# The order of turns, products and copies in the mixer stages of a two-layer encoder kernel

## What is computed

```python
def _chunk_relpos_core(q, k, v, q_pos, k_pos, valid, table):   # layer 0, mixer A, 8 heads
    s = jnp.einsum('bcqhd,bckhd->bchqk', q, k) * ATTN_SCALE + bias[None, None]
    p = jax.nn.softmax(jnp.where(valid[None, :, None, None, :], s, NEG_INF), axis=-1)
    return jnp.einsum('bchqk,bckhd->bcqhd', p, v)

def _diff_core(q, k, v, q_pos, k_pos, lam, slopes):            # layer 0, mixer B, 4 double heads
    s = jnp.einsum('bqhid,bkhid->bhiqk', q, k) * ATTN_SCALE - slopes * dist
    p = jax.nn.softmax(jnp.where(vis, s, NEG_INF), axis=-1)
    return jnp.einsum('bhqk,bkhd->bqhd', p[:, :, 0] - lam * p[:, :, 1], v)

def _forget_core(q, k, v, dq, dk, q_pos, k_pos):               # layer 1, mixer C, 16 heads
    s = jnp.einsum('bqhd,bkhd->bhqk', q, k) * ATTN_SCALE + dq - dk
    p = jax.nn.softmax(jnp.where(k_pos <= q_pos, s, NEG_INF), axis=-1)
    return jnp.einsum('bhqk,bkhd->bqhd', p, v)

proj = h @ w_in      # gives q, k and v of each head; k and v are outputs too (new cache rows)
out  = concat(heads) @ w_out
```

## Time and profile before

| | before |
|---|---|
| median of 3 runs | 2443.89 us (2441.65 to 2446.6) |
| profiled execution | 2447.24 us |
| its span on the core | 2445.4 us |
| mean granted TensorE clock | 0.987 of 2.4 GHz |
| PE busy | 2337.1 us (96% of the span) |
| DVE busy | 1443.2 us (59%) |
| ACT busy | 907.9 us (37%) |

### The profile page before, as it was taken

How to read it: one execution, slowest core, us unless ns; L and a number is a source line. 1 busy time by engine, 2 the same in 40 slices (tenths; PEclk the granted TensorE clock), 3 DMA queues, 4 the chain that set the end, 5 groups by cost and what they waited for, 6 DMA issues and landing times.

```text
span 2445.4 us, 45688 instructions
## 1 busy us (share of the span) xinstructions
PE 2337.1 (96%) x18984; PEld 2224.9 (91%) x18984; DVE 1443.2 (59%) x2606; ACT 907.9 (37%) x1964; POOL 305.0 (12%) x369
## 2 busy tenths in 40 slices
PE   7999999999997999999999999997999899999998
PEld 4999999978776999999999999996777789999998
DVE  4577757655557756657575665756555576543223
ACT  4322232455555422223342222334555564222232
POOL 0000002411103400001220000233011151000001
PEclk9999999999998999999999999998999999999999
DMA  7455546322222135445524454542233221432321
GB/s 244 125 165 172 165 131 169 102 71 74 76 64 75 51 114 154 139 136 153 143 61 130 138 156 130 154 124 64 79 98 98 81 87 53 138 104 87 97 85 56
DMA packets 392701, 277.68 MB, mean 114 GB/s; under 512 B 11104, under 2 KB 349824, under 8 KB 392496
## 3 DMA queue, kind: packets, MB, share of 16 engines
q1 hardware_dynamic: 385792, 254.77, 35.5%
q0 software_dynamic: 6704, 19.99, 2.8%
HBM read 263.48 MB, written 12.81 MB: 113 GB/s over the span
## 4 chain that ended last, share of the span: by engine, by line
PE 83%; DVE 8%; ACT 3%; issue 3%; DMA 2%; POOL 1%; SPq 0%; ACTq 0%; DVEq 0%; POOLq 0%
PE lin L1018 61%; PE lin L1275 9%; PE lin L1038 2%; PE ps_s L1325 2%; PE ps_o L1397 2%; PE ps_t L1346 1%; DVE neg_max L2416 1%; DVE acc L1981 1%; DMA raw<-in_ffn_w_down 1%; DVE x L2066 1%; DVE probs L2408 1%; PE ps_s L1094 1%; DVE sums L2028 1%; DVE h_lo L2093 1%; ACT w_hi L1513 0%
## 5 line engine op out<-in xcount | busy, mean ns | idle before, releaser
L1018 PE MATMUL lin<-h_hi,w_hi 128*128 128x272 f32 x2640 | 566.4, 289 | 4.0 <-ACT work L1593 2.1
L1018 PE MATMUL lin<-h_hi,w_lo 128*128 128x272 f32 x2640 | 563.6, 289 | 0.0
L1018 PE MATMUL lin<-h_lo,w_hi 128*128 128x272 f32 x2640 | 561.5, 288 | 0.0
L1942 DVE TENSOR_TENSOR w_lo<-raw,w_hi 128x1024 fp32r<-128x1024 f32 (+1 forms) x263 | 320.5, 1223 | 309.8 <-ACT w_hi L1513 308.1
L1018 PEld LDWEIGHTS lin<-h_hi,w_hi 128*128 128x128 f32 x2640 | 421.2, 188 | 6.6 <-ACT work L1593 2.8
L1018 PEld LDWEIGHTS lin<-h_lo,w_hi 128*128 128x128 f32 x2640 | 421.6, 189 | 0.0
L1018 PEld LDWEIGHTS lin<-h_hi,w_lo 128*128 128x128 f32 x2640 | 418.9, 189 | 0.0
L1513 ACT ACTIVATE w_hi<-raw 128x1024 fp32r<-128x1024 f32 (+1 forms) x263 | 270.1, 1037 | 182.5 <-DMA raw<-in_ffn_w_down 143.5
L1981 DVE SCALAR_TENSOR_TENSOR acc<-raw,silu_c,acc 128x512 f32<-128x512 f32 x448 | 314.0, 759 | 0.0
L1018 PE MATMUL lin<-act_hi,w_hi 128*128 128x272 f32 x1296 | 285.1, 290 | 5.6 <-DVE w_lo L1942 5.3
L1018 PE MATMUL lin<-act_lo,w_hi 128*128 128x272 f32 x1296 | 283.0, 289 | 0.0
(11 more groups left out here) (313 smaller groups left out, 3461.1 us busy)
## 6 DMA issues: line engine op xcount, KB each, us to landing
raw<-in_w_ada SPq DMA_DIRECT2D x128, 512.0 KB, 3.9
raw<-in_ffn_w_gate SPq DMA_DIRECT2D x88, 512.0 KB, 3.9
raw<-in_ffn_w_up SPq DMA_DIRECT2D x88, 512.0 KB, 3.8
raw<-in_ffn_w_down SPq DMA_DIRECT2D x64, 448.0 KB, 4.3
raw<-in_ffn_w_down SPq DMA_DIRECT2D x32, 512.0 KB, 5.0
raw<-in_w_in_ab SPq DMA_DIRECT2D x24, 512.0 KB, 3.8
raw<-in_w_in_c SPq DMA_DIRECT2D x24, 512.0 KB, 3.8
start_w<-in_w_ada SPq DMA_DIRECT2D x16, 512.0 KB, 12.0
```

What stands on the lines that cost most here:

```text
L1018: m = nc.tensor.matmul(out[a], w_tile(w, k), mv[:, k0 + k, half(a)], start=first and k == 0 and n == 0, stop=last and k == u["tiles"] - 1 ...
L1942: nc.vector.tensor_tensor(w_all(w_l, u["tiles"]), raw_all(u, w_l), w_all(w_h, u["tiles"]).bitcast(F32), ALU.subtract).then_inc(lo_done, 1)
```

## The change

Three things change, in the order of instructions alone; no instruction is added, removed or resized.

1. In stages 1 to 7 the turns go from the start of steps 5, 9 and 12 to the end of steps 5, 9 and 11, on PE and on ACT. On PE a turn now stands behind the step's product, softmax transposes and value products. On ACT its copies now stand behind the step's `out_hi`, `inv_copy` and `empty_probs`, ahead of its exponential; for the rest that puts them ahead of step 12 and so of `evac(2)`, the copy of qT.
2. `tr_plan` counts the turn behind the softmax block of the same step.
3. In stage 0 the turn of v goes to bank `ps_o`, without a wait for `tr_out`; the turn of the rest then waits only for the copy of k.

```diff
+TURN_STEPS = (5, 9, 11)
@@ tr_plan
             for s in range(STEPS + 2):
-                if st.new is not None and s in (5, 9, 12):
-                    found.append((s, "turn"))
                 j = s - lag
                 if st.att is not None and 0 <= j < 10 and (st.att != "b" or j % 2):
                     found.append((s, "probs"))
+                if st.new is not None and s in TURN_STEPS:
+                    found.append((TURN_STEPS.index(s), "turn"))
             return found
+        def turn_bank(st, i):
+            return ps_o if st.st == 0 and i == 1 else ps_t
@@ PE, turn
-                    n = tr_plan(st).index((step, "turn"))
-                    wait_tr(base + n)
-                    if step in (5, 9):
+                    n = tr_plan(st).index((i, "turn"))
+                    if turn_bank(st, i) is ps_t:
+                        wait_tr(base + (1 if st.st == 0 and i == 2 else n))
+                    if i < 2:
                         for t in range(QT):
-                            m = nc.tensor.transpose(ps_t[:, t * P:(t + 1) * P], src[:, t * P:(t + 1) * P], ident[:])
+                            m = nc.tensor.transpose(turn_bank(st, i)[:, t * P:(t + 1) * P], src[:, t * P:(t + 1) * P],
+                                                    ident[:])
@@ PE, a step
-                    if st.new is not None and s in (5, 9, 12):
-                        turn(s)
...
                     if att != "b" and 0 <= j < 10 and j % 2:
                         pair_values(j // 2)
+                    if st.new is not None and s in TURN_STEPS:
+                        turn(TURN_STEPS.index(s))
                     if s < 10 and s % 2 == 0:
                         scores(s)
                         scores(s + 1)
@@ ACT, a step
                     if st.new is not None:
                         if s in (4, 8, 12):
                             evac(s // 4 - 1)
-                        if s in (5, 9, 12):
-                            empty_turn(s)
...
                     if 0 <= j < 10 and j % 2 and att == "b":
                         b_square(j // 2)
+                    if st.new is not None and s in TURN_STEPS:
+                        empty_turn(TURN_STEPS.index(s))
                     if s < 10:
                         exps(s)
```

More of the change, by code:

```diff
@@ L1414, in stage @@
                         m.then_inc(fl_ps, 1)
-                    for s in (5, 9, 12):
-                        turn(s)
+                    for i in range(3):
+                        turn(i)
                     return
                 for s in range(STEPS + 2):
-                    if st.new is not None and s in (5, 9, 12):
[L1421 to L1431, removed]
+                    if st.new is not None and s < LIN_STEPS:
+                        lin_chunk(s, 0)
+                        lin_chunk(s, 1)
+                    if st.st == 8 and s in OUT_PART[st.kind]:
+                        m, k = OUT_PART[st.kind][s]
+                        if k == 0:
+                            pe.wait_ge(kv_evac, evs)
+                        if k == max(OUT_PART[st.kind].values())[1]:
+                            pe.wait_ge(o_lo_done, st.at("ot"))
+                        out_part(st.j, m, k)
                     j = s - lag
@@ L1793, in first_stage @@
                 split(("q", j, 1, 0))
-                for s in (5, 9, 12):
-                    empty_turn(s)
+                for i in range(3):
+                    empty_turn(i)
             def forget_act():
@@ L1813, in evac, with empty_turn @@
                                          scale=HD ** -0.5 if k == 2 else 1.0).then_inc(kv_evac, 1)
-                def empty_turn(step):
-                    n = plan_t.index((step, "turn"))
+                def empty_turn(i):
+                    n = plan_t.index((i, "turn"))
                     act.wait_ge(tr_ps, st.at("tr") + n + 1)
-                    if step in (5, 9):
-                        if step == 5:
+                    if i < 2:
+                        if i == 0:
                             act.wait_ge(kv_stored[st.new], 64 * st.same_new)
-                        dst = (k_nat if step == 5 else v_nat)[:, st.new, 0:QT, :].rearrange("p t n -> p (t n)")
-                        nc.scalar.activation(dst, ps_t[:, :], ACT.Copy).then_inc(tr_out, 1)
+                        dst = (v_nat if i else k_nat)[:, st.new, 0:QT, :].rearrange("p t n -> p (t n)")
+                        nc.scalar.activation(dst, turn_bank(st, i)[:, :], ACT.Copy).then_inc(tr_out, 1)
                     else:
@@ L1832, in empty_probs @@
                         act.wait_ge(pv_done, st.at("pv") + (q - 1 if att == "b" else q // 2))
+                    dst = probsT[:, q % 2]
                     if t < QT:
-                        nc.scalar.activation(probsT[:, q % 2, 0:t + 1, :].rearrange("p b n -> p (b n)"),
+                        nc.scalar.activation(dst[:, 0:t + 1, :].rearrange("p b n -> p (b n)"),
                                              ps_t[:, 0:(t + 1) * P], ACT.Copy).then_inc(tr_out, 1)
                     else:
-                        nc.scalar.activation(probsT[:, q % 2, 0:2, 0:DEC],
+                        nc.scalar.activation(dst[:, 0:2, 0:DEC],
                                              ps_t[:, 0:2 * P].rearrange("p (b n) -> p b n", b=2)[:, :, 0:DEC], ACT.Copy)
-                        nc.scalar.activation(probsT[0:DEC, q % 2, 2, 0:DEC], ps_t[0:DEC, 2 * P:2 * P + DEC], ACT.Copy)\
+                        nc.scalar.activation(dst[0:DEC, 2, 0:DEC], ps_t[0:DEC, 2 * P:2 * P + DEC], ACT.Copy)\
                             .then_inc(tr_out, 1)
```

8 lines of the change are left out of this document (4 added, 4 removed).

## The result

| | before | after |
|---|---|---|
| median of 11 runs each | 2444.9 us | 2452.67 us |
| lowest and highest | 2441.65 to 2448.11 | 2445.78 to 2463.28 |
| profiled execution | 2447.24 us, granted clock 0.987 | 2460.93 us, granted clock 0.984 |

The ratio is 1.0036 with a 95% interval of 1.0023 to 1.0049: the change makes the kernel slower, by 7.8 us from median to median. The forecast was 2452.0 with a range of 2444.5 to 2459. The profiled execution lies above that range, which is a first hint that something varies from run to run.

The account below looks back on a forecast made before the run. PE, busy 96% of the span, was taken to bound the kernel. Terms +4.8 + 7.4 - 4.6 - 0.9 = +6.7 us on the median 2443.89 gave 2450.6; one clock fall of 1.7 made 2452, range 2444.5 to 2459.

Parts of the forecast that it names:

- The ends: Ends of "a" and "c" stages: next product waits for qT, copied later; +0.69 us at ten, +0.5 at one, +7.4 in all.
- Steps 5 and 9: In 11 "a" and "c" stages: turns wait for the `probsT` copy, +0.22 us per step, +4.8 in all.
- ACT's lateness: Step 5 of "a" and "c" stages: ACT reaches its copy only at 1788.17, behind a weight split begun at 1787.65.
- "b" stages: Stages 2, 4, 6 of layer 0: the wait ahead of the turn of k goes, 3 x 1.53, -4.6 us.
- Stage 0: Layer 0: turn of v no longer waits for `k_nat`, next product starts earlier, -0.9 us; layer 1: 0.
- The sum at full clock: Whole kernel, four order terms without any added clock fall: +6.7 us, giving 2450.6 on the median.
- The clock: Ends of "a" and "c" stages: a longer stretch of short work and waits may let the granted clock fall, 1.7 us each.
- one fall of the clock, 1.7, which is likelier than none: Added to the 2450.6 us of the order terms: a single fall of the granted clock, 1.7 us, giving 2452.
- The rival at 2459: A third to a half of the 11 "a" and "c" ends lose clock, +7 to +8 us, about 2459; chance 0.17.
- a mean clock under 0.98: Sign in the measured profile: mean clock below 0.98 would put the rival of many clock falls first.
- Steps free: Steps 5 and 9 of "a" and "c" cost nothing, as earlier `o_hi` repays: sum +1.9, 2446 us; chance 0.15.
- the loop through `o_hi`: Earlier `o_hi` at steps 5 and 9 paces "a" and "c" stages, gaining 10.6 us: sum -8.7, 2435; chance 0.08.

Follow-up runs that it names:

- Experiment 5: Kernel before with only ACT's copies of the turned rest put ahead of qT's copy at stage ends, one bank: 2455.78 us, ratio 1.0038.
- experiment 1: Changed kernel with ACT's copy of qT put back ahead of the three copies of the turned rest: 2442.89 us, ratio to before 0.9993.
- experiment 4: Kernel before with only the turns of k and v in "a" and "c" stages moved to the end of steps 5 and 9: 2449.19 us, ratio 1.0017.
- filled kernel: Changed kernel plus four unused matmuls on PE behind the last value products of "a" and "c" stages, filling the wait for qT: 2450.77 us, ratio 1.0025.
- experiment 6: The changed kernel again, unaltered, on another chip, against the kernel before: 2456.46 us, ratio 1.0040.
- experiment 2: Kernel before with only the "b" stages' turns of k and v moved to the end of steps 5 and 9, single bank in stage 0: 2437.41 us, ratio 0.9974.
- experiment 8: Kernel before with ACT's k and v copies at the end of steps 4 and 8 in "a"/"c", changed "b" stages and stage 0 bank: 2419.18 us, ratio 0.9891.

## Why the prediction was right, and where it was not

**The ends: right.** Predicted +0.69 each. Experiment 5, with nothing else changed, has +0.72, and experiment 1, with nothing else taken back, -0.73. At stage 7 of layer 0 and behind the last "c" stage waits of 0.6 stand, where 0.5 and 0.69 were forecast. The durations came out of the trace's rows; by the formula of the Trainium skill ("ScalarE: Activation LUTs", section "What ACT_TABLE_LOAD costs") the term was 0.84, and the measured 0.72 to 0.73 decides for the rows. With ten ends and a half it is +7.7 against +7.4.

**Steps 5 and 9: right.** Predicted +0.44 for a stage, measured 0.40 (experiment 4), so +4.4 against +4.8. The turn of k waits 1.13, where 1.1 to 1.3 was said. The copy of 384 columns takes 0.47, estimated at 0.49. With the two terms a "c" stage was to last 35.9 us, and at full clock it lasts 35.87. One reading was too short: the prediction puts ACT's lateness on the weight split ahead of the copy, but ahead of both stood an exponential that waited 1.26 us for DVE's `neg_max`. In the change it waits the same 1.26 us, so the sum did not suffer.

**"b" stages: right.** -1.51 measured, -1.53 predicted for a stage. The kernel with that part alone is 6.8 faster where 4.6 was forecast; the interval holds both, and one or two falls fewer would fill the gap.

**Stage 0: right.** From the turn of k to the next product it is 497.87 - 494.95 = 2.92 us, before 3.85: -0.9. In layer 1 the wait for `decay` did grow, to 4.2 us.

**The sum at full clock** is thus 4.4 + 7.7 - 4.5 - 0.9 = +6.7, the forecast's own value. The filled kernel measures that sum without the falls at the ends: 0.0025 of 2444.25 is +6.1 (3.9 to 8.3).

**The clock: right mechanism, mis-sized term.** The step "one fall of the clock, 1.7, which is likelier than none" treated falls as rare and separate. A fall costs 37.41 - 35.87 = 1.54 us, close to 1.7. Their number is what was off: 0, 3, 6 and 6 at the six counted ends of layer 1. By the ratios the change costs about 8.8 us (0.0036 of 2444.9), 2 to 3 more than the 6.1 of the filled version; from median to median it is 7.8 and 6.5. On the chip of experiment 6 the change cost 9.8 by the ratio. So I estimate the share of the clock at 1 to 4 us, and that the 1.7 falls into it is in part luck: it was one fall, and there are none or several. The intervals of 1.0036 and 1.0025 overlap, so the size of the clock's share in the median is an estimate. That PE standing still at the end lets the clock fall rests on counts of "c" stages behind a fall: 16 of 30 where the wait is there (the change and experiment 5, five executions), 0 of 18 where it is filled (three), and 0 of 30 where there is none (before and experiments 1, 2, 4 and 8). Falls of one execution are not independent of each other. By executions it is 4 of 5 with at least one such fall, against 0 of 3 and 0 of 5; taken alone, the change against its filled version is 3 of 4 against 0 of 3, which is thin. The spread of 8.0 us of the filled version's ten runs against 17.5 supports it, though the six runs of the change in experiment 6 lie as close (7.4). What decides whether a given end falls is open. The rival at 2459 describes single executions (2460.93, 2461.41), not the median. The sign by which I meant to tell it, a mean clock under 0.98, was set wrong too: six falls bring it only to 0.984.

The Trainium skill ("TensorE: Matmul & The Clock Gate", section "Part 1: The HAM clock gate") says that activity releases the throttle and that the point at which the clock rises varies from run to run. It says so of the rise at the start of steady work; the four profiles of the change show as much variation in falls, 0 to 6 from one list of instructions.

**The other rivals fell.** "Steps free" and "the loop through `o_hi`" would have had experiment 4 at +0 or below; it is +0.40 per stage and 1.0017. ACT's lateness is in part DVE's, as the first of them had it, but it stayed: the exponential starts 1789.24 - 1787.21 = 2.03 us behind the scores in the change, 2.04 before.

## What to carry to other kernels

When two engines hand one bank to and fro, look first at the place of the copy in the copying engine's own list: with PE's order untouched in "a" and "c", moving ACT's copies ahead of an exponential and a weight split gave most of 1.1%, while moving the turns there behind the softmax block cost 0.17%. A copy that sits in a hole of its engine is free (qT before, k in experiment 8), and the same copy three places later can hold up the next stage (0.72 us, ten times over). So look for the rows in which the copying engine waits for a third one. And where a stage ends in small matmuls, a fraction of a microsecond of waiting more can, in some executions, cost the clock twice that again, so compare several profiles, stage by stage, before a difference of 0.3% is explained.

## What was not expected of the hardware

- The clock fell behind waits well under a microsecond between short matmuls. The end of a "c" stage has no wait above 0.67 us, and the clock fell behind it in 15 of 24 cases (in three of four executions); with that wait filled by four matmuls it fell in 0 of 18 (three executions).
- Falls came in rows. They stood behind all six ends in a row, or behind three in a row and then none. With a fall a stage is 37.4 us long, without one 35.87; whether the changed spacing itself keeps the falls coming was not tried.
- A wait that is taken away gives back more than the idle time printed ahead of its row: 1.98 us for 1.61 in two waits of experiment 8, and 0.67 printed at the end of a stage for 0.72 to 0.73 lost. The ends of matmuls are modelled, and I take the idle time to be counted from a modelled end. The view by window fits: the "c" stage of the earlier trace rows has PE busy for 32.44 us, and one of experiment 8, with the same matmuls at the same clock, for 32.07. The difference of 0.37 is just what 1.98 has over 1.61.

```profile
1718.55:1751.31 32.76, 32.07 (x279) 27.34 (x279) 19.04 (x56) 18.53 (x57) 5.16 (x8) 1.00 0.34 100
```
